# Forgetting attention: the inverse row sums reach all partitions by transfers inside SBUF instead of by matrix products, and a tile's closing multiplication moves one group later

## The reference, cut to what matters

```python
s = jnp.einsum('bqhd,bkhd->bhqk', q[:, q0:kend], k[:, :kend]) * scale
s = s + c[:, :, q0:kend, None] - c[:, :, None, :kend]
p = jax.nn.softmax(jnp.where(mask[None, None], s, NEG_INF), axis=-1)
outs.append(jnp.einsum('bhqk,bkhd->bqhd', p, v[:, :kend]))
```

## Time and profile before

| what | value |
|---|---|
| device time, three executions | 2922.24 us median (2921.28 to 2925.21) |
| span of the profiled execution, first to last instruction | 2924.8 us |
| TensorE busy | 2840.5 us (97%) |
| DVE busy | 1712.9 us (59%) |
| ACT busy | 616.3 us (21%) |
| POOL busy | 1350.4 us (46%) |

### The profile page before, as it was taken

The page is one execution under the profiler, slowest core; times in us unless marked ns, Lnnn a source line. Parts: engine busy times, 40 slices in busy tenths (PEclk is TensorE's granted clock), DMA queues, the critical chain, the costliest instruction groups (busy, mean ns, idle before and its releaser), DMA issues.

```text
span 2924.8 us, 40628 instructions
## 1 busy us (share of the span) xinstructions
PE 2840.5 (97%) x14442; PEld 2069.8 (71%) x14442; DVE 1712.9 (59%) x4617; ACT 616.3 (21%) x1269; POOL 1350.4 (46%) x1140
## 2 busy tenths in 40 slices
PE   8999999999999999998999989999999999999997
PEld 4478888888875555554455767878877777777775
DVE  6665656656346767674677534777677773332326
ACT  2221212110025454552110100011111111111114
POOL 3433534447730110101355335677667666555645
PEclk9999999999999999999999999999999999999999
DMA  6500110101121103014435456889989989999986
GB/s 219 184 6 1 31 45 1 30 15 44 30 77 35 63 30 129 28 33 170 173 137 159 131 198 197 270 277 277 271 277 289 291 271 302 305 304 305 317 258 254
DMA packets 192571, 470.49 MB, mean 161 GB/s; under 512 B 27384, under 2 KB 108104, under 8 KB 166632
## 3 DMA queue, kind: packets, MB, share of 16 engines
q1 hardware_dynamic: 145424, 347.63, 33.3%
q0 software_dynamic: 44640, 111.84, 16.5%
q10 hardware_dynamic: 2304, 8.39, 0.7%
HBM read 349.64 MB, written 118.11 MB: 160 GB/s over the span
## 4 chain that ended last, share of the span: by engine, by line
PE 39%; DMA 6%; DVE 3%; POOL 2%; issue 2%; SPq 1%; another core or an unknown queue 0%; ACT 0%; DVEq 0%; POOLq 0%; ACTq 0%
PE ps L3021 18%; PE ps L2796 6%; DMA moe_xg<-t_rows,index 5%; PE ps L2969 4%; PE ps L2940 3%; PE ps L2852 2%; DVE moe_xT L2097 2%; PE ps L2937 2%; POOL moe_xg L2523 1%; PE ps L2862 1%; PE ps L2815 1%; POOL moe_fin L2605 1%; PE ps L2806 0%; DMA base_rows<-moe_yo,index 0%
## 5 line engine op out<-in xcount | busy, mean ns | idle before, releaser
L2523 POOL DMA_INDIRECT moe_xg<-t_rows,index x433 | 428.6, 990 | 174.7 <-issue 139.2
L3021 PEld LDWEIGHTS ps<-moe_xT,moe_wg 128*128 128x128 f32 x2048 | 352.5, 196 | 54.6 <-issue 31.3
L3021 PE MATMUL ps<-moe_xT,moe_wg 128*128 128x192 f32 (+22 forms) x2048 | 380.0, 338 | 9.3 <-DVE moe_hh L1997 5.4
L3021 PE MATMUL ps<-moe_xT,moe_wu 128*128 128x192 f32 (+22 forms) x2048 | 376.3, 337 | 0.0
L3021 PEld LDWEIGHTS ps<-moe_xT,moe_wu 128*128 128x128 f32 x2048 | 354.2, 197 | 4.8
L2544 POOL DMA_INDIRECT base_rows<-moe_yo,index x100 | 231.0, 2310 | 273.2 <-DVE moe_yo L2111 116.8
L2097 DVE STREAM_TRANSPOSE moe_xT<-moe_xg 128x256 f32<-128x256 f32 x433 | 235.1, 610 | 174.2 <-DMA moe_xg<-t_rows,index 155.9
L1296 POOL TENSOR_TENSOR fox_diag<-fox_c,fox_causal 128x128 f32<-128x128 f32 x128 | 55.8, 457 | 450.9 <-DVE fox_mx L1325 446.1
L2660 ACT ACTIVATE moe_sl<-ps 128x256 f32<-128x256 f32 (+19 forms) x144 | 49.6, 345 | 953.9 <-PE ps L3021 736.8
L1997 DVE TENSOR_TENSOR moe_hh<-moe_sl,ps 128x256 f32<-128x256 f32 (+19 forms) x144 | 49.7, 358 | 292.4 <-ACT moe_sl L2660 194.9
L1319 DVE CUSTOM_DVE_ANT_0 hT<-ps,fox_c 128x512 f32<-128x512 f32 (+7 forms) x320 | 166.3, 560 | 63.0 <-PE ps L1581 62.7
(11 more groups left out here) (373 smaller groups left out, 5052.1 us busy)
## 6 DMA issues: line engine op xcount, KB each, us to landing
moe_wg<-in_we_gate SPq DMA_DIRECT2D x64, 1024.0 KB
moe_wu<-in_we_up SPq DMA_DIRECT2D x64, 1024.0 KB
moe_wd<-in_we_down SPq DMA_DIRECT2D x64, 1024.0 KB
fox_c<-ck SPq DMA_DIRECT2D x8, 1032.0 KB, 8.9
emb_xin<-in_x SPq DMA_DIRECT2D x16, 512.0 KB, 3.9
h_rows<-emb_hr SPq DMA_DIRECT2D x16, 512.0 KB, 2.7
ret_w<-in_w_in SPq DMA_DIRECT2D x16, 512.0 KB, 6.6
moe_yt<-h_rows SPq DMA_DIRECT2D x16, 512.0 KB
```

Of the source, the lines that this page charges most:

```text
L2523: pool.indirect_dma_start(out=xg[g % NXG][:, :], out_offset=None, in_=quarters, in_offset=bass.IndirectOffsetOnAxis(ap=route.index4[:, AT4 ...
L3021: ins = pe.matmul(out, w[:, c, f:FF:FC], xT[u][:, c, 0:n], start=(c == 0), stop=(c == DC - 1))
```

## The change: the division by transfers

After the change `inverse(n)` stops at the reciprocal. In the last step of a tile, TensorE also transposes the 128x4 reciprocals into four rows (an otherwise unused part of the step's PSUM bank); ACT copies these four rows to `rT`, ahead of the copy of that step's probabilities. SP then issues four transfers from SBUF to SBUF, each of which repeats one row of 128 numbers over 64 partitions of `rB`. `scatter`, `rd`, the ones and `keep` go. `finish(n)` waits for the transfers and stands in round 2 of the next tile instead of round 1 (in the last round where there are fewer). The store of tile n moves to SP's turn of tile n + 1, ahead of that tile's four transfers.

```diff
+            def inverse_rows(n):
+                b = n % 2
+                sp.wait_ge(rT_set, n + 1)
+                if n >= 2:
+                    sp.wait_ge(scaled, n - 1)
+                for q in range(2):
+                    for a in range(2):
+                        sp.dma_start(rB[b][FD * a:FD * (a + 1), P * q:P * (q + 1)],
+                                     rT[b][2 * q + a:2 * q + a + 1, :].unsqueeze(1).to_broadcast([1, FD, P])).then_inc(rB_in[b], 16)
...
             for n, (p, t) in enumerate(order):
                 if n in TURN_AT:
...
-                sp.wait_ge(scaled, n + 1)
-                sp.dma_start(foxT[2 * FD * p:2 * FD * (p + 1), QT * t:QT * (t + 1)], oT[n % 2][:, :]).then_inc(o_s[n % 2], 16)
-                if (n + 1) % TILES == 0 and p + 2 < PAIRS:
-                    pair_values(p + 2)
-                    pair_gates(p + 2)
+                if n >= 1:
+                    store(n - 1)
+                if n >= 1 and n % TILES == 0 and p + 1 < PAIRS:
+                    pair_values(p + 1)
+                    pair_gates(p + 1)
+                inverse_rows(n)
+            store(NT - 1)
...
                 dve.reciprocal(rinv[b][:, :], rs[b][:, :]).then_inc(inverted, 1)
-                dve.wait_ge(inverted, n + 1)
-                for r in range(4):
-                    ins = dve.tensor_scalar(rd[b][:, r, :], ident[:, :], rinv[b][:, r:r + 1], None, ALU.mult)
-                ins.then_inc(rd_set, 1)
...
             def finish(n):
                 b = n % 2
-                dve.wait_ge(spread_c, n + 1)
+                dve.wait_ge(weighed, step0[n + 1])
+                dve.wait_ge(rB_in[b], 64 * (n // 2 + 1))
...
-                    if i == 1 and n >= 1:
+                    if i == min(2, max(len(groups[n]), lead[n]) - 1) and n >= 1:
                         finish(n - 1)
...
                 elif s == steps[n] - 1:
+                    if n >= 2:
+                        act.wait_ge(scaled, n - 1)
+                    nc.scalar.copy(rT[n % 2][:, :], src[0:4, 0, :]).then_inc(rT_set, 1)
                     ins = nc.scalar.copy(dst[:, 1:4:2, :], src[:, 1:4:2, :])
...
-            def keep(n):
-                b = n % 2
-                act.wait_ge(spread, n + 1)
-                if n >= 2:
-                    act.wait_ge(scaled, n - 1)
-                nc.scalar.copy(rB[b][:, :], ps[:, O0 + b, QT:2 * QT]).then_inc(spread_c, 1)
...
+                        if ss[0] == steps[n] - 1 and a == 0:
+                            pe.wait_ge(inverted, n + 1)
+                            pe.transpose(ps[0:4, T0 + g % 2, 0:P], rinv[n % 2][:, :], ident[:, :])
...
-            def scatter(n):
-                pe.wait_ge(rd_set, n + 1)
-                if n == 0:
-                    pe.wait_ge(ones_set, 1)
-                for q in range(2):
-                    for a in range(2):
-                        ins = pe.matmul(ps[FD * a:FD * (a + 1), O0 + n % 2, QT + P * q:QT + P * (q + 1)], onesf[:, :],
-                                        rd[n % 2][:, 2 * q + a, :], start=True, stop=True)
-                ins.then_inc(spread, 1)
```

More of the change, by code:

```diff
@@ L1174, in fox_phase @@
         diag = [sb(f"diag{b}", [P, P]) for b in range(4)]
-        onesf = sb("onesf", [P, FD])
         mx = [sb(f"mx{b}", [P, 2, 8]) for b in range(4)]
@@ L1186, in fox_phase @@
         pT = [sb(f"pT{b}", [P, 4, P]) for b in range(4)]
-        rd = [sb(f"rd{b}", [P, 4, P]) for b in range(2)]
+        rT = [sb(f"rT{b}", [4, P]) for b in range(2)]
         rB = [sb(f"rB{b}", [P, QT]) for b in range(2)]
@@ L1190, in fox_phase @@
         zero = lambda name: ph.zero_sems(name, 1)[0]
-        tab, ones_set = ahead.fox_tab, zero("ones_set")
+        tab = ahead.fox_tab
         w_s, v_s, c_s = ahead.fox_w, ahead.fox_v, ahead.fox_c
@@ L1203, in fox_phase @@
         turned, pT_a, pT_d, weighed = (zero(n) for n in ("turned", "pT_a", "pT_d", "weighed"))
-        inverted, rd_set, spread, spread_c, scaled = (zero(n) for n in ("inverted", "rd_set", "spread", "spread_c", "scaled"))
+        inverted, rT_set, scaled = (zero(n) for n in ("inverted", "rT_set", "scaled"))
+        rB_in = ph.zero_sems("rB_in", 2)
         block = yield
@@ L1262, in _, with store @@
             pair_gates(1)
+            def inverse_rows(n):
[7 more added lines that the diff above has]
+                                     rT[b][2 * q + a:2 * q + a + 1, :].unsqueeze(1).to_broadcast([1, FD, P])).then_inc(rB_in[b], 16)
+            def store(n):
+                p, t = order[n]
+                sp.wait_ge(scaled, n + 1)
+                sp.dma_start(foxT[2 * FD * p:2 * FD * (p + 1), QT * t:QT * (t + 1)], oT[n % 2][:, :]).then_inc(o_s[n % 2], 16)
             for n, (p, t) in enumerate(order):
@@ L1284, in _ @@
                     fox_token_sum(pool, ahead, hT, g, part)
-            pool.memset(onesf[:, :], 1.0).then_inc(ones_set, 1)
             pool.wait_ge(tab, 16)
@@ L1346, in back @@
                 elif s == steps[n] - 1:
+                    dve.tensor_copy(rT[n % 2][:, :], src[0:4, 0, :]).then_inc(rT_set, 1)
                     ins = dve.tensor_copy(dst[:, 1:4:2, :], src[:, 1:4:2, :])
@@ L1355, in inverse @@
                 if n >= 2:
-                    dve.wait_ge(spread, n - 1)
+                    dve.wait_ge(turned, step0[n - 1])
                 dve.reciprocal(rinv[b][:, :], rs[b][:, :]).then_inc(inverted, 1)
-                dve.wait_ge(inverted, n + 1)
-                for r in range(4):
-                    ins = dve.tensor_scalar(rd[b][:, r, :], ident[:, :], rinv[b][:, r:r + 1], None, ALU.mult)
-                ins.then_inc(rd_set, 1)
             def turn_rows(m, g):
@@ L1516, in _ @@
                         exps(n + 1, q, a)
-                    if i == 0 and n >= 1:
-                        keep(n - 1)
-            keep(NT - 1)
         @block.tensor
@@ L1673, in _ @@
                         scores(n + 1, u)
[L1674 to L1680, removed]
-                    else:
-                        scatter(n)
-                        for u in (range(first[n + 2]) if n + 2 < NT else []):
-                            scores(n + 2, u)
-                        for s in after:
-                            turn(n + 1, s)
+                if not early:
+                    for u in (range(first[n + 2]) if n + 2 < NT and order[n][1] else []):
+                        scores(n + 2, u)
+                    for s in after:
+                        turn(n + 1, s)
         yield
```

## The result

The changed kernel takes 2939.2 us, the kernel before 2925.9 (medians of 12 runs each): ratio 1.0046, 95% interval 1.0035 to 1.0058, so 13.3 us slower. The forecast was 2930 with a range of 2917 to 2942. The profiled execution has a span of 2936.5 us against 2924.8.

The account below looks back on a forecast made before the run. TensorE was taken to bound attention, busy 486.1 of 513 us. Ends of tiles -4.3, tile 17 +4.4 and the end +8.1 gave +8.2 us on the median of 2922.24: 2930 us, range 2917 to 2942.

Parts of the forecast that it names:

- the two waits: Places where the transfers aren't covered: DVE waits for the broadcast rows behind tile 17 (4.4 us) and at attention's end (8.1).
- The end, +8.1: Attention's end: two chains of transfers, tiles 30 and 31, one behind the other, delay the last store by 8.1 us.
- T: Time from first issue to last landing of a tile's four transfers; taken as 6 us, between 3.9 and 10.
- Tile 17, +4.4: Tile 17's transfers stand behind 4.5 MB of loads; DVE waits 4.4 us at `finish(17)`, passed on whole to TensorE.
- T - 1.4 - 1.9: Time from the queue emptying at 1172.1 to the landing of tile 17's four transfers, at 1174.8 for T = 6.
- The ends of tiles, -4.3: Scatter's products gone, a transposition added: -0.99 us per pair for three pairs, -1.30 for the last, -4.3 in all.
- The later place of `finish` itself costs DVE nothing: Moving `finish` to the next tile's third round costs DVE 0; SP's store is a round later and nobody waits.
- t = 1 and 0: Last two tiles of a pair: reciprocals come late in t = 0, its scatter's removal gives nothing; together they lose 0.31 us.
- quick transfers: Rival: the four transfers take T = 3.9, sum +1.9 us, 2924 us, no difference; chance 0.31.
- one after the other: Rival: the four transfers run in a row, T = 10, with a clock fall +22.8 us, 2945 us; chance 0.15.
- the faster one: Rival: TensorE's saving of 0.39 us counts in all 32 tiles, with T = 3.9 -6.3 us, 2916 us; chance 0.12.
- One source for all four: Forecast's upper part: neighbouring partitions share what reads them, T = 7, +11.2 us, 2933 us; 0.12 of the forecast's chance.

Follow-up runs that it names:

- before_late: Kernel before with only the last multiplication moved to its later place, scatter and its copy kept; ratio 1.0012 to the kernel before.
- all_mended: Changed kernel with last two tiles spread the old way, weights behind tile 17's broadcasts, broadcasts ahead of next pair's loads, multiplication at round 1; 0.9987 of the kernel before.
- two_queues: Changed kernel with two of the four broadcasts issued by ScalarE and two by SyncE in the last two tiles; ratio 1.0041 to the kernel before.

## Why the prediction came out as it did

The direction and the two waits were right, the saving was not there, and the median came 9 us above the forecast, inside the range. Of these 9 us, about 4 are the kernel before, whose twelve executions have a median of 2925.9 where the forecast started from 2922.24; the change itself cost 13.3 us instead of 8.2.

*The end, +8.1.* Measured 8.75, with the two chains where they were forecast, and T = 6.3 for the 6 that was chosen between 3.9 and 10. The estimate that the prediction takes from the Trainium skill, T = 6.6, missed by as much on the other side.

*Tile 17, +4.4.* One DVE wait, in tile 18, passed on to TensorE as forecast, but a shorter one: 1.50 us here, and 1.50 to 3.04, 2.4 on average, in the eight profiles that have these weights, this wait and the later multiplication. The step that was too large is T - 1.4 - 1.9: it puts the last of the four 2.7 us behind the landing of a store in the same full queue, and it came 0.8 behind it (1174.2 and 1175.0). Besides, this profile's tile 18 began 3.4 us late, so DVE came to its multiplication at 1173.6 instead of 1170.4. What the tile adds to the lag is 1.64 us here and 1.64 to 5.52, 3.9 on average, in the eight. After TensorE waits of 2.35, 2.50 and 3.24 us the clock stayed up there; after the five from 3.33 to 3.90 it fell, and these five are the dear ones, at 4.29 us and more. The prediction saw this edge and left the clock's part out. So 3.9 beside 4.4 is in part luck: as an estimate, 2.6 of it is the wait (where the clock stayed up, the tile adds 0.7 less than TensorE's wait) and 1.3 the clock.

*The ends of tiles, -4.3.* Measured zero, and the prediction's own test (the first two pairs 1 us shorter each) failed. The step that failed is the sentence "The later place of `finish` itself costs DVE nothing". DVE had the time, but not at that place: in the t=6 and t=5 tiles the multiplication went ahead of a copy that TensorE already waited for, and this is nearly all of the 2.5 us that the later place costs (before_late). Without it the saving is real but smaller: 2.5 us (all_mended), per pair 0.88 for t = 7 to 2 where 1.30 was forecast. There a transposition costs 0.08 us instead of 0.14, but a scatter gone gives 0.35 instead of 0.53, so both together 0.27 instead of 0.39. For t = 1 and 0 the forecast was met, part by part: -0.39 and +0.70, +0.31 together.

*Not forecast: the clock at the pair ends.* The wait there trebled, and the clock fell at 7 of 24 places: at up to 1.6 us each, 7 x 1.6 / 8 profiles = 1.4 us per execution.

The sum in these sizes: 0 + 3.9 + 8.75 + 1.4 = 14 us, against 13.3 measured, with an interval of 10 to 17. It is averaged over profiles of several kernels, so the agreement is no proof of each term.

Of the rivals, quick transfers (T = 3.9) and one after the other (T = 10) are excluded by T; the faster one failed: even with the transfers hidden and the early place a scatter gone gives 0.27 us, not 0.39, and the t=0 tiles lose what the profile's rows said they might. One source for all four was right in its mechanism: from partitions 0 to 3 the rows share one way out, at 6.3 where it took 7.

## What to carry to other kernels

An instruction that is moved within a queue can cost up to its duration to whoever waits for what stands behind it, however idle its engine is on average, and can give time back at its old place: here 0.42 us of DVE cost 0.25 to 0.43 in three tiles of a pair and gave 0.33 back in a fourth. Look up what is released behind both places. Transfers that are hidden elsewhere were paid where nothing was left to hide them, at the end of the phase in full and behind a bulk load in the same queue in part: keep the old way for those tiles, and issue the small transfer ahead of the bulk.

## What the runs showed of the hardware beyond that

- A broadcast of one 512-byte row to 64 partitions (32 KB) takes SP 0.6 us to issue. Two of them can be used 3.9 us after the first issue (two_queues), four after 6.3 if all four rows lie on partitions 0 to 3, and after 4.6 from partitions 0, 4, 8 and 12. Behind 4.5 MB of loads in the same queue each landed 8.5 to 8.9 us after its issue.
- TensorE's clock went to its lower level behind a wait of only 1.5 us in 7 of 24 places and stayed up in 17; in attention's first tile it fell in 3 of 14 profiles with the same waits, 1.21 and 0.44 us. In tile 18 it fell after all six waits of 3.33 to 5.16 us, for 3 to 7 us, and after none of the three of 2.35 to 3.24.
